# Two residual blocks on one core: w_out by seven products, an earlier state half, and another split of the later one-hots

## The reference, cut to what matters

```
xn = rmsnorm(h); proj = xn @ w_in
mixed = sigmoid(g1) * conv_module(...) + sigmoid(g2) * gated_linear_attention(...)
h = h + mixed @ w_out                    # 256 x 2048 times 2048 x 2048
q = rmsnorm(h) @ peer_wq                 # product keys: 16 experts of 16384 for each of 8 heads
h = h + sum over experts of gate * gelu(u . xn) * v
h = rmsnorm(h); second block: delta rule and cross attention, then x = x + y @ w_out_2
```

## Time and profile before

| | |
|---|---|
| median of three runs | 3664.84 us (3664.70 to 3669.83) |
| the profiled execution | 3664.0 us |
| its span, first to last instruction | 3662.3 us |
| TensorE busy, share of the span | 98% |
| VectorE, ScalarE, GpSimd busy | 56%, 17%, 27% |
| mean granted TensorE clock | 0.992 |

### The profile page before, as it was taken

How to read it: one execution, slowest core, us unless ns; L and a number is a source line. 1 busy time by engine, 2 the same in 40 slices (tenths; PEclk the granted TensorE clock), 3 DMA queues, 4 the chain that set the end, 5 groups by cost and what they waited for, 6 DMA issues and landing times. The chain is left out here.

```text
span 3662.3 us, 51124 instructions
## 1 busy us (share of the span) xinstructions
PE 3577.6 (98%) x20754; PEld 3164.9 (86%) x20754; DVE 2058.6 (56%) x4109; ACT 621.3 (17%) x1423; POOL 976.2 (27%) x813
## 2 busy tenths in 40 slices
PE   8999999999999999999898999999999999999999
PEld 6878887899998888888787777777799999999988
DVE  4883102055540399865698544444466766676653
ACT  0002202100002112221167100000222222222100
POOL 0000100101000156675886555455100112222000
PEclk9999999999999999999999999999999999999999
DMA  5433432344444699999895899999533422221352
GB/s 217 140 137 138 143 134 81 116 161 172 188 184 183 237 333 401 404 409 362 290 349 200 314 336 331 347 335 331 183 139 125 150 99 99 99 99 70 141 197 111
DMA packets 159014, 776.65 MB, mean 212 GB/s; under 512 B 19476, under 2 KB 21420, under 8 KB 122812
## 3 DMA queue, kind: packets, MB, share of 16 engines
q1 hardware_dynamic: 100536, 518.52, 38.8%
q0 software_dynamic: 57344, 251.69, 18.4%
q10 hardware_dynamic: 900, 3.17, 0.3%
HBM read 762.67 MB, written 10.64 MB: 211 GB/s over the span
## 5 line engine op out<-in xcount | busy, mean ns | idle before, releaser
L405 PE MATMUL PS<-mem,ring 128*128 128x272 f32 (+1 forms) x2816 | 645.0, 392 | 3.0 <-DMA ring<-in_first_tiles 3.0
L405 PEld LDWEIGHTS PS<-mem,ring 128*128 128x128 f32 x2816 | 539.7, 192 | 106.1 <-issue 4.6
L1281 POOL DMA_INDIRECT mem<-in_peer_ug,idx x256 | 358.0, 1398 | 535.1 <-DVE idx L1795 346.4
L1933 DVE SCALAR_TENSOR_TENSOR mem<-mem 128x768 f32<-128x768 f32 x256 | 261.3, 1021 | 286.8 <-DMA mem<-in_peer_vg,idx 280.8
L1848 DVE CUSTOM_DVE_ANT_0 mem<-mem 128x1152 f32<-128x1152 f32 x256 | 348.4, 1362 | 96.7 <-DMA mem<-in_peer_ug,idx 96.5
L1395 PE MATMUL PS<-mem 128*128 128x256 f32 x1792 | 387.5, 379 | 1.7 <-DMA mem<-in_peer_ud 1.6
L1395 PEld LDWEIGHTS PS<-mem 128*128 128x128 f32 x1792 | 340.2, 190 | 48.6 <-DMA mem<-in_peer_ud 2.5
L1307 POOL DMA_INDIRECT mem<-in_peer_vg,idx x256 | 281.3, 1099 | 281.4 <-DVE mem L1933 232.1
L413 PEld LDWEIGHTS PS<-mem,ring 128*128 128x128 f32 x3136 | 350.3, 192 | 0.1
L413 PE MATMUL PS<-mem,ring 128*128 128x128 f32 x3136 | 350.3, 275 | 0.0
L2279 PE MATMUL PS<-mem,ring 128*128 128x128 f32 x2560 | 312.3, 275 | 0.9 <-issue 0.6
(11 more groups left out here) (413 smaller groups left out, 4467.0 us busy)
## 6 DMA issues: line engine op xcount, KB each, us to landing
ring<-in_first_tiles SPq DMA_DIRECT2D x144, 1024.0 KB, 4.8
ring<-in_dn_tiles SPq DMA_DIRECT2D x88, 1024.0 KB, 5.3
mem<-in_peer_vd SPq DMA_DIRECT2D x128, 640.0 KB, 6.9
mem<-in_peer_ud SPq DMA_DIRECT2D x128, 448.0 KB, 6.8
ring<-in_out_panels SPq DMA_DIRECT2D x16, 2048.0 KB, 8.3
ring<-in_w_out SPq DMA_DIRECT2D x8, 2048.0 KB, 9.0
ring<-in_peer_wq SPq DMA_DIRECT2D x8, 2048.0 KB, 8.0
mem<-second_keys SPq DMA_DIRECT2D x64, 256.0 KB, 5.2
```

The costliest lines, as they stand in the source:

```text
L405: last = nc.tensor.matmul(PS[:, 4 + n % 4, 0:T if wide else TX], wslots[slot_of[n]][:, k, :], x, start=(k == 0), stop=(k == KT - 1))
L1281: nc.gpsimd.indirect_dma_start(ugs[at % US], None, a["peer_ug"], bass.IndirectOffsetOnAxis(ap=idx[:, n, j:j + 1], axis=0)).then_inc(u_in[a ...
L1933: nc.vector.scalar_tensor_tensor(hc, Vg[:, at % GS, :], dots[:, m, h * PTOP + j:h * PTOP + j + 1], hc, ALU.mult, ALU.add).then_inc(vg_used, 1)
```

## The change

It has three parts.

1. w_out: panels go in four pairs. For each pair the 256 x 2048 by 2048 x 512 product is cut into 2 x 2 parts (token halves, halves of the 2048, the two panels), and seven products of half the depth take the place of eight. Before the first, VectorE makes three sums of the turned operand and overwrites one part with a fourth; for each pair it makes four sums of weights, of which one overwrites a weight part, and twelve small instructions that put the products together in `h_tok`. A pair's two slots are given free together, by its last product. The transposes of h stand in the next pair; the memory's stand in the third and fourth pair, four parts behind each other. h is squared behind, all into one scratch row, each instruction after the one before.
2. `state(1, 0)` stands ahead of the products with the faded q and k.
3. VectorE makes the second one-hot of the later tokens with n % 4 == 0, ScalarE those with n % 4 == 2.

```diff
                     o_inverse(0)
+                    state(1, 0)
                     dve.wait_ge(exps, 10)
                     q_mul(1, qs)
                     ks_mul(1, 0)
                     ks_mul(1, 1)
                     dve.wait_ge(exps, 11)
                     q_mul(1, qe)
-                    state(1, 0)
                     state(1, 1)
...
-                        pe.wait_ge(h_added, 2 * p + 2)
+                        pe.wait_ge(h_added, 4 * (p // 2) + 4)
...
+                    def wo_product(j, x, w):
+
+                        for k in range(KH2):
+                            last = nc.tensor.matmul(wo_bank(j), x[:, k, :], w[:, k, :], start=(k == 0), stop=(k == KH2 - 1))
+                        if j < WON:
+                            last.then_inc(wo_done, 1)
+                        else:
+                            last.then_inc(tile_ready, 2 * TPP)
+
+                    for g in range(RING):
+                        b11, b21, b12, b22 = wo_weights(g)
+                        s, turn = 2 * g % RING, 16 * (G_WO // RING + 1 + 2 * g // RING)
+                        pe.wait_ge(slot_loaded[s], turn)
+                        if g:
+                            pe.wait_ge(wo_chain, WO_LINKS * (g - 1) + 3)
+                        wo_product(0, wo_x[0, 0], b11)
+                        wo_product(1, wo_x[0, 1], b21)
+                        if g:
+                            h_transposes(2 * g - 2)
+                            pe.wait_ge(wo_chain, WO_LINKS * (g - 1) + 6)
+                        else:
+                            pe.wait_ge(wo_operands, 4)
+                        pe.wait_ge(slot_loaded[s + 1], turn)
+                        wo_product(2, wo_s4, b22)
+                        pe.wait_ge(wo_sums, 4 * g + 1)
+                        wo_product(3, wo_s1, wo_t1)
+                        if g:
+                            h_transposes(2 * g - 1)
+                            pe.wait_ge(wo_chain, WO_LINKS * (g - 1) + 8)
+                        pe.wait_ge(wo_sums, 4 * g + 2)
+                        wo_product(4, wo_x[1, 0], b12)
+                        pe.wait_ge(wo_sums, 4 * g + 3)
+                        wo_product(5, wo_s2, wo_t2)
+                        if g >= 2:
+                            for n in range(4 * g - 8, 4 * g - 4):
+                                mem_transposes(n)
+                        if g:
+                            pe.wait_ge(wo_chain, WO_LINKS * g)
+                        pe.wait_ge(wo_sums, 4 * g + 4)
+                        wo_product(6, wo_x[1, 1], wo_t4)
...
                                 if n == 0:
-                                    if k == 8:
-                                        h_transposes(2 * RING - 1)
+                                    if k in (4, 8):
+                                        h_transposes(2 * RING - 2 + k // 8)
...
-                        elif n % 8:
-                            pe.wait_ge(hot_act, P + 3 * ((n - P) // 8) + n % 8 // 2)
+                        elif n % 4:
+                            pe.wait_ge(hot_act, P + (n - P) // 4 + 1)
...
-                        second_hot(n + 4)
...
+                    def wo_operand_sums():
+
+                        nc.vector.tensor_tensor(wo_s1, wo_x[1, 0], wo_x[1, 1], ALU.add).then_inc(wo_operands, 1)
+                        dve.wait_ge(wo_operands, 1)
+                        nc.vector.tensor_tensor(wo_s2, wo_s1, wo_x[0, 0], ALU.subtract).then_inc(wo_operands, 1)
+                        nc.vector.tensor_tensor(wo_x[1, 0], wo_x[0, 0], wo_x[1, 0], ALU.subtract).then_inc(wo_operands, 1)
+                        dve.wait_ge(wo_operands, 2)
+                        nc.vector.tensor_tensor(wo_s4, wo_x[0, 1], wo_s2, ALU.subtract).then_inc(wo_operands, 1)
...
+                        nc.vector.tensor_tensor(wo_t1, b12, b11, ALU.subtract).then_inc(wo_sums, 1)
+                        dve.wait_ge(wo_sums, sums + 1)
+                        nc.vector.tensor_tensor(b12, b22, b12, ALU.subtract).then_inc(wo_sums, 1)
...
+                        nc.vector.tensor_tensor(wo_t2, b22, wo_t1, ALU.subtract).then_inc(wo_sums, 1)
...
+                        nc.vector.tensor_tensor(wo_t4, wo_t2, b21, ALU.subtract).then_inc(wo_sums, 1)
...
+                    wo_operand_sums()
+                    for g in range(RING):
+                        wo_weight_sums(g)
                         if g == 1:
                             dve.wait_ge(m_roots, 1)
                             nc.vector.reciprocal(ssm[:, 0, :], ssm[:, 1, :]).then_inc(m_scale, 1)
+                        wo_evict(g)
...
-                        if m and n % 8 == 0:
+                        if m and n % 4 == 0:
                             nc.vector.tensor_scalar(second_of(n), iota[:, :], turnk[:, m, 1, t:t + 1], None, ALU.is_equal)
```

More of the change, by code:

```diff
@@ L1003, in flat, with wo_bank, wo_weights @@
             return t.rearrange("p k n -> p (k n)")
+        WON, WO_LINKS = 6, 12
+        wo_x = {(m, f): mixT[:, f * KH2:(f + 1) * KH2, m * P:(m + 1) * P] for m in range(MT) for f in range(2)}
+        wo_s1, wo_s2, wo_s4 = spot(29440, KH2, P), spot(MEM + 2048, KH2, P), spot(22784, KH2, P)
+        wo_t1, wo_t2, wo_t4 = spot(27392, KH2, PW), spot(MEM, KH2, PW), spot(20736, KH2, PW)
+        wo_c1, wo_u2, wo_u3 = (spot(23808 + PW * j, PW) for j in range(3))
+        sq_junk = spot(24576, PW)
+        def wo_bank(j):
+            return PS[:, j // 2, (j % 2) * PW:(j % 2 + 1) * PW]
+        def wo_weights(g):
+            s = 2 * g % RING
+            return ring[:, s, 0:KH2, :], ring[:, s, KH2:KT, :], ring[:, s + 1, 0:KH2, :], ring[:, s + 1, KH2:KT, :]
         HN, US, GS, VS, OS, LO = MT * PH, 6, 4, 4, 4, 16
@@ L1020, in xn_t @@
             return xnD[:, k, :] if k < KU else xnR[:, k - KU, :]
-        sq_tok, memT = spot(20736, MT, D), spot(4096, KT, TX)
+        memT = spot(4096, KT, TX)
         def score_t(n):
@@ L1539, in mem_evict @@
                                                  scale=pcol("mem_norm_g_2", 2 * n + k)).then_inc(mt_out, 1)
-                    for p in range(2 * RING):
-                        if p == 1:
+                    for g in range(RING):
+                        if g == 0:
                             act.wait_ge(m_in, 32)
@@ L1553, in _ @@
                                                      scale=ssm[:, 0, m:m + 1]).then_inc(m_scaled, 1)
[L1554 to L1562 removed]
+                        if g:
+                            for p in (2 * g - 2, 2 * g - 1):
+                                h_evict(p)
+                                h_square(p)
+                            if g >= 2:
+                                for n in range(4 * g - 8, 4 * g - 4):
+                                    mem_evict(n)
+                    for p in (2 * RING - 2, 2 * RING - 1):
+                        h_square(p)
+                    for p in (2 * RING - 2, 2 * RING - 1):
+                        h_evict(p)
                     act.wait_ge(h_sum, 1)
@@ L1712, in _ @@
                     dve.wait_ge(x_in, 32)
-                    for p in range(2 * RING):
-                        if p == 2:
+                    def wo_operand_sums():
[5 more added lines that the diff above has]
+                        nc.vector.tensor_tensor(wo_s4, wo_x[0, 1], wo_s2, ALU.subtract).then_inc(wo_operands, 1)
```

86 lines of the change are left out of this document (51 added, 35 removed).

## The result

| | before | after |
|---|---|---|
| median of four runs each, same chip | 3666.3 us | 3641.2 us |
| range | 3664.7 to 3669.8 | 3640.5 to 3644.7 |
| profiled execution, its span | 3664.0 us, 3662.3 us | 3641.8 us, 3640.0 us |

The ratio is 0.9931, 95% interval 0.9917 to 0.9945: faster by 25 us. The prediction said 3640, range 3632 to 3649.

The account below looks back on a forecast made before the run. TensorE, busy 98%, was taken as the bound. The terms -9.7 - 9.2 - 5.6 = -24.5 us, from the profiled 3664.0, gave 3639.5, stated as 3640 us with a range of 3632 to 3649.

Parts of the forecast that it names:

- Part 1: w_out by seven products: -13.7 for one panel less, +2.0 for product boundaries, +2.0 for transpose stalls, together -9.7 us.
- 0.07 a product, x 28 = +2.0: w_out: each of 28 products, a group of its own with waits ahead, costs TensorE 0.07 us more, +2.0 us.
- The stall at the memory's transposes: w_out: TensorE waits for ScalarE to empty the first bank, 1.0 us in each of two batches, +2.0 us.
- The store: Store of the residual behind one more panel on SP's queue: 4.9 us later, covered by VectorE's 6.28 idle with 1.4 left.
- rival B: Store of the residual lands too late and holds the search and gathers, at most 4.9 us: 3645; chance 0.07.
- Part 2: Second chunk's state half added ahead: TensorE's 6.65 us idle and 2.54 us of low clock go, -9.2 us.
- Rival C: State: TensorE's wait moves on to ScalarE's fade or the second half, giving back up to 6.65: 3647; chance 0.04.
- Part 3: One-hots of the later tokens: 32 tokens take 11.3 instead of 12.72 us, -1.4 four times, -5.6 us.
- The group is VectorE's now: One-hot stage: VectorE bounds each eight tokens at 2.74 us, ScalarE falls to 2.23, GpSimd stays at 2.49.
- Rival A: One-hot trade gives nothing, VectorE held by the dense product or GpSimd held up: 3646, up to 3647.5; chance 0.17.
- Nothing behind absorbs it: Behind w_out: gathers and dense work both start from its end, TensorE paces both weight streams, so the -24.5 us stays.
- Rival D: Slower: new stops in w_out bring TensorE to 1.2 GHz and it stays there, 95.8 us more: 3736; chance 0.02.

Follow-up runs that it names:

- e4_mem_spread: Changed kernel with the memory's four transposes of a pair split two and two, behind products 4 and 5: 3638.7 us, ratio 0.9921.
- e7_store_first: Changed kernel with the store of the residual ahead of the third and fourth panel of the queries' weights on SP's queue: 3641.6 us, one run.
- e11_changed_again: Changed kernel once more, nothing altered, beside a version without the one-hot change on one chip: 3638.9 us, ratio 0.9909.
- e6_early_gathers: Changed kernel with three gathers of V rows and their additions moved into the stage of the one-hots: 3642.4 us, ratio 0.9934.
- e2_wout_only: Kernel before with only w_out by seven products, state line and one-hots as before: 3653.6 us, ratio 0.9952.
- e3_hot_only: Kernel before with only the new split of the later tokens' one-hots: 3666.6 us, ratio 0.9990.

## Why the prediction was right, step by step

- **Part 1, predicted -9.7, measured -11.2** (-11.0 alone). The removed panel counted right. "0.07 a product, x 28 = +2.0" was mis-sized: a product boundary costs nothing that shows here. 7 x 3.42 + 2 x 0.55 = 25.04 against the 25.05 of the second pair. The 0.07 was no overhead: it set a distance of two starts (6.91) against half of a panel's busy time (6.84). Two w_out products behind each other start their 32 instructions 6.91 apart too (1120.44 and 1127.35). The stall at the memory's transposes, 1.0 forecast in each batch, is 1.16, and `e4_mem_spread` showed its cause, the second use of two banks, by taking it away. (The 0.3 us for handing a bank over in that sum came from no row.) The range's lower end subtracts 3.1 and 2.0 by its words, but its 3632 is 2.0 and 2.0 below 3636. Sums, panels and squares are hidden, as said.
- **The store** was forecast to leave VectorE 1.4 us; it left 1.38, in part by luck. From the last addition of w_out to VectorE's products behind the store it is 18.3 us where it was 14.3, so 4.0 more and not 4.9, and to the search 22.7 where it was 23.6. `e7_store_first` moved the store and not the search, so rival B fails by that margin.
- **Part 2, predicted -9.2, measured -9.4** in place. The low clock of the eight products went with the wait, 2.6 us of it. Rival C didn't come: no wait of TensorE for L877 is left. Of the gain 1.6 us came back as low clock behind the state in this profile; that is not the change's doing, as the same stretch is 465.1 to 468.4 us in runs with this part and 466.8 to 468.4 without.
- **Part 3, predicted -5.6.** The stage itself gave -6.7: the beat is 11.0, not 11.3. VectorE's group of eight took 2.55 (two of 1.27), not 2.74, and the stall was mis-sized the other way, 11.0 - 4 x 2.55 = 0.8 and not 0.3. "The group is VectorE's now" fits the rows: behind the dense product TensorE runs off its store for nine tokens and then waits in short steps. But VectorE, GpSimd (10.05 + 0.9) and TensorE fill the beat so nearly alike that no run here tells which of them alone sets it. Rival A is refuted in the stage by three profiles (44.0, 44.1, 44.4).
- **"Nothing behind absorbs it" is the step that failed.** Nearly half of part 3 is given back: of 6.6 us nine profiles keep 3.5 at the end of y's turn and 3.6 at the end of the span. Two things do it. VectorE used to be 2.3 us ahead of TensorE at the end of the stage (first V-row addition 2019.7, last table product 2022.0) and now is 0.3 ahead (1996.9, 1997.2), so the gathers' chain starts only 4.7 us earlier of 6.7. And that chain isn't made shorter by TensorE being early: with the DMA engines at 94% it takes 550.1 us on the mean in the four profiles without the part and 552.7 in the five with it, so the last V-row addition comes 2.0 us earlier and no more. Why the chain grew is not shown; that TensorE's dense weights take more of the same engines' time would fit. The profile before had the evidence: 2.29 us of wait for the row scales, so the gathers' path ended last already, with both paths full ahead of it. I had looked for what starts late, not for what would end last.
- **Rival D** (the clock in w_out) didn't come: the low clock at its start cost 2.0 us (8.88 for 32 instructions, 6.88 later), 1.7 before.
- That the total is within 1.2 us of the median is luck in part. Part 1 was 1.5 better, part 3 about 2 worse, and the low clock fell in other places; in `e11_changed_again` the same kernel was at 0.9909 of the one before, not 0.9931.
- The rule of the Trainium skill, "SBUF — State Buffer", section "Who interferes with whom", was weighed with rival A. The trace speaks against it here more clearly than before: VectorE's 2.55 us and GpSimd's 2.51 (10.05 / 4) of each eight tokens lie in 2.75 (11.01 / 4). Whether VectorE's one-hots ran in the two-port mode no row shows, and for VectorE's addition of V rows beside a GpSimd one-hot the runs do show one engine held up by the other (0.83 us in `e6_early_gathers`).

## What to carry to other kernels

Before work is moved off the engine that bounds a stage, look at the next place where two paths meet: the wait there says which ends last and by how much. What the path that waits gains alone is lost; only what the other path gains as well is kept. A small gap of an engine takes in only what is shorter than the gap, counted with what the moved work does to its neighbours (a one-hot of 0.60 us took 1.43 beside the moved addition). A row without a bracket is not yet an engine without waits: compare its pace with the pace right after it had stood still. Where an instruction waits both for a place and for its turn, put other work ahead of the wait, not behind it. An overhead of 0.07 us, read from one pair of start times, should not be multiplied by 28 without a second row.

## What the runs showed that I had not expected

**The same code runs at another clock from one execution to the next.** Up to 600 us all kernels here are the same. Windows of 500 to 600 us, changed kernel, then `e2_wout_only` (behind the engines: granted clock, DMA share, GB/s):

```profile
500.00:600.00 100.00, 100.00 (x523) 81.21 (x522) 14.41 (x49) 9.65 (x15) 0.00 (x0) 0.97 0.33 116
```
```profile
500.00:600.00 100.00, 100.00 (x506) 82.36 (x505) 14.41 (x49) 9.24 (x13) 0.00 (x0) 0.90 0.30 104
```

At a granted 0.90 instead of 0.97 TensorE gets 17 instructions less done in the same 100 us. A product of a tile (32 instructions) behind short products takes 7.17 us in one execution and 9.38 in another (the one at 537.2 and at 539.3 us). In ten profiles of kernels that are the same up to there, the last instruction of the state starts between 623.1 and 631.1 us. Such a spread of 8 us is as large as what one part of this change gives, so the parts were measured by stretches of the trace and not by totals; `e2_wout_only` and `e3_hot_only` began w_out 7.5 and 4.0 us later than the kernel before, with no change ahead of it. What sets the clock in these places was not tried.
